# Key pages past the projection: products written to PSUM, pages released by VectorE alone

## The chip, the cores and the metric

One core of a Trainium2 chip runs the whole program; nothing is shared with other cores. The metric is the device time of one execution in microseconds. The kernel before takes 2161.31 us (median of 3 runs, 2160.24 to 2163.03). In the text TensorE is PE in the profile's rows, VectorE is DVE, ScalarE is ACT, GpSimd is POOL and SyncE is SP.

## The reference, cut to what matters

The reference runs one step of a 4-layer decoder trunk for a prompt of 256 tokens and 8 sample sequences that share all weights. Only the attention layer (layer 1) is touched, and of it only the sample side. Each of the 8 samples has one new query of 8 heads x 128 values and 8 past pages of keys (128 positions x 8 heads x 128). What the stretch around the change computes is

```
for n in 8 samples, j in 8 pages, h in 8 heads:
    score[n, j, position, h] = sum over d of key[page_table[n, j], position, h, d] * q[n, h, d]
```

Behind it the page scores are summed by blocks of 256 keys, the three best blocks are kept, a softmax is taken, and the value pages are weighted by it.

## The kernel before, in words

All engines run hand-written queues, tied by semaphores that only count up. The layer projects the input to q, k and v in 12 steps (stage qkv, TensorE). The 64 key pages (t = 8n + j) are loaded one by one by DMAs that GpSimd issues (lines 1323 to 1363): it waits for a free buffer, reads the page's number from the table into a register, and starts a transfer of 512 KB into one of 8 SBUF buffers, pg0 to pg7. A page's 128 positions lie on the 128 partitions, its 8 x 128 values along the free dimension. TensorE spreads the query of sample n over all partitions of two PSUM banks, A[n % 2].

`key_scores(t)` on VectorE (line 1762 on) waits for the page (`s_pg[j]`), multiplies heads 0 to 3 by the query in one instruction (line 1768, counted in `s_km`), and does heads 4 to 7 with one multiply-and-sum each (line 1770, the last counted in `s_kd`). `key_sums(t)` on ScalarE (line 1056 on) waits for `s_km` and sums the products of heads 0 to 3 with four copies that also accumulate (line 1060, the last counted in `s_ka`). Products, and the by-products of the multiply-and-sum, are written over the page itself. After every eighth page VectorE drains, waits until ScalarE has summed this last page, and copies the 64 sums away (line 1776).

A page's buffer is loaded again once both `s_kd` and `s_ka` have counted it (lines 1333 and 1334), so page t follows page t - 8. The eighth sample's key pages (56 to 63) are loaded behind four value pages that go to buffers of their own (pgx). Value pages then reuse the ring.

Pages 0 to 10 are scored between the steps of the projection (`keys_after`, line 346); pages 11 to 63 follow when it is over, one after the other. Two PSUM tensors of two banks each, G[0] and G[1], hold the projection's results, then the rows of k and v of the samples, which ScalarE copies out (`s_row` reaches 3), and lie unused until the scores are complete (`s_kall`, line 1788). TensorE then transposes the scores, and everything else in the layer follows from that.

Of the kernel before, what the change touches and what calls it, by code (L numbers as in the profile page):

```python
# [21 lines left out]
ALU = mybir.AluOpType  # L22
ACT = mybir.ActivationFunctionType
# [3 lines left out]
P = 128  # L27
# [3 lines left out]
NB = 8  # L31
# [13 lines left out]
PAGES = 8  # L45
PGX = 4
# [27 lines left out]
def build_trunk(nc, t_in, t_out):  # L74
# [3 lines left out]
    with ctx:  # L78
# [3 lines left out]
        def sem(name):  # L82
            return ctx.enter_context(nc.semaphore(name))
# [5 lines left out]
        h = sb("h", [P, KT, T])  # L89
# [40 lines left out]
        def row(off, items):  # L130

            got = {}
            for name, shape, *dt in items:
# [4 lines left out]
                if off < x1 and off + n > x0:  # L138
# [46 lines left out]
        pg, m2 = row(m1, [(f"pg{j}", [P, MH, P]) for j in range(PAGES)])  # L185
# [3 lines left out]
        ms, m4 = row(x1, [("sR", [64, 1056]),  # L189
                          ("qk", [P, NB, MH]), ("gsum", [64, BLOCKS]), ("geq", [64, BLOCKS]),  # L190
                          ("gsc", [64, 8]), ("bco", [P, 64]),
                          ("sq0", [P, PAGES, MH]), ("sq1", [P, PAGES, MH])])
# [32 lines left out]
        G = [ctx.enter_context(nc.psum_tensor(f"G{p}", [P, 2, 512], F32)) for p in range(2)]  # L225
# [51 lines left out]
        s_rowT, s_row, s_qbc = sem("s_rowT"), sem("s_row"), sem("s_qbc")  # L277
        s_km, s_ka, s_kd = sem("s_km"), sem("s_ka"), sem("s_kd")
# [67 lines left out]
        def keys_after(r):  # L346

            return range(max(0, 2 * r - 13), 2 * r - 11) if r >= 6 else range(0)

        def mix_count(i):  # L350

# [511 lines left out]
        def _(act):  # L863
            fn = nc.scalar.activation
# [186 lines left out]
            def moba():  # L1051
                def query_rows(j, src):
                    act.wait_ge(s_rowT, j + 1)
                    fn(M["rowS"][:, j, :], src[0:NB].rearrange("b a n -> b (a n)"), ACT.Copy).then_inc(s_row, 1)

                def key_sums(t):
                    n, j = t // PAGES, t % PAGES
                    act.wait_ge(s_km, t + 1)
                    for hh in range(4):
                        f = fn(pg[f"pg{j}"][:, hh, :], pg[f"pg{j}"][:, hh, :], ACT.Copy, accum_out=ms[f"sq{n % 2}"][:, j, hh:hh + 1])  # L1060
                    f.then_inc(s_ka, 1)

                def beside_qkv(r, u):
                    if r == 4:
                        query_rows(0, A[0])
                    for t in keys_after(r):
                        key_sums(t)
                splits(stage[1, "qkv"], beside_qkv, norm=3)
                query_rows(1, G[0])
                query_rows(2, G[1])  # L1070
                for t in range(keys_after(11)[-1] + 1, NB * PAGES):
                    key_sums(t)
                act.wait_ge(s_sR, 1)
                fn(ms["sR"][:, 0:1025], ms["sR"][:, 0:1025], ACT.Exp, scale=SCALE, bias=ms["gsc"][:, 2:3],
                   accum_out=ms["gsc"][:, 3:4]).then_inc(s_sE, 1)

                def weigh(hh):
                    act.wait_ge(s_msc, hh + 1)
                    b = hh % 2
                    sc, nm, rs = mh[f"sc{b}"], mh[f"nm{b}"], mh[f"rs{b}"]  # L1080
                    fn(sc[:, 0:P], sc[:, 0:P], ACT.Exp, scale=SCALE, bias=nm[:, 0:1], accum_out=rs[:, 0:1])
                    fn(sc[:, P:3 * P], sc[:, P:3 * P], ACT.Exp, scale=SCALE, bias=nm[:, 1:2], accum_out=rs[:, 1:2]).then_inc(s_mex, 1)

                def turned(hh):
                    act.wait_ge(s_mpT, hh + 1)
                    if hh >= 2:
                        act.wait_ge(s_mo, hh - 1)
                    fn(mh[f"pt{hh % 2}"][:], pt_bank[:, 0:3 * P], ACT.Copy).then_inc(s_mpt, 1)

                def summed(n):  # L1090
                    act.wait_ge(s_vd, 4 * PAGES * (n + 1))
                    fn(vO[n][:].rearrange("p h d -> p (h d)"), A[n][:].rearrange("p a n -> p (a n)"), ACT.Copy).then_inc(s_vo, 1)
                weigh(0)
                for hh in range(MH):
                    if hh == 4:
                        summed(0)
                    turned(hh)
                    if hh + 1 < MH:
                        weigh(hh + 1)
                act.wait_ge(s_att, 1)  # L1100
                fn(ao["oH"][:, :, 0:SEQ], M["att"][:, :, 0:SEQ], ACT.Copy).then_inc(s_mixh, 1)
                summed(1)
                act.wait_ge(s_att, 2)
                fn(ao["oH"][:, :, SEQ:T], M["att"][:, :, SEQ:T], ACT.Copy).then_inc(s_mixh, 1)
                splits_out(stage[1, "wo"], 4)
# [110 lines left out]
        def _(pool):  # L1216
            gp = nc.gpsimd
# [104 lines left out]
            def moba():  # L1322
                pool.wait_ge(s_ev, stage[1, "qkv"]["c0"])
                pool.dma_start(ptab[:], t_in["page_table"].rearrange("b j -> (b j)").unsqueeze(0)).then_inc(s_tab, 16)
                pool.wait_ge(s_tab, 16)

                def page(pool_dram, t, buf, landed):
                    pid = pool.value_load(ptab[0:1, ds(t, 1)], min_val=0, max_val=pool_dram.shape[1] - 1)
                    pool.dma_start(buf[:], pool_dram[0][ds(pid, 1)].rearrange("o t h d -> t (o h) d")).then_inc(landed, 16)

                def key_page(n, j):
                    if not (isinstance(n, int) and n == 0):
                        pool.wait_ge(s_kd, n * PAGES + (j - 7))
                        pool.wait_ge(s_ka, n * PAGES + (j - 7))
                    page(t_in["cache_k"], n * PAGES + j, pg[f"pg{j}"], s_pg[j])

                def value_page(turn, s):

                    if isinstance(turn, int) and turn == 0:
                        if s >= PGX:  # L1340
                            pool.wait_ge(s_kd, PAGES * (NB - 1) + s - PGX + 1)
                            pool.wait_ge(s_ka, PAGES * (NB - 1) + s - PGX + 1)
                    else:
                        pool.wait_ge(s_vd, turn * RING + (s - RING + 1))
                    page(t_in["cache_v"], turn * RING + s, ring[s], s_px[s] if s < PGX else s_pg[s - PGX])
                for j in range(PAGES):
                    key_page(0, j)
                with gp.Fori(1, NB - 1) as it:
                    for j in range(PAGES):
                        key_page(it, j)  # L1350
                pool.wait_ge(s_mm, stage[1, "qkv"]["g0"] + 12)
                for s in range(PGX):
                    value_page(0, s)
                for j in range(PAGES):
                    key_page(NB - 1, j)
                for s in range(PGX, RING):
                    value_page(0, s)
                turns = NB * PAGES // RING
                with gp.Fori(1, turns) as it:
                    for s in range(RING):  # L1360
                        value_page(it, s)
                for s in range(NB * PAGES - turns * RING):
                    value_page(turns, s)
# [42 lines left out]
        def _(dve):  # L1406
            V = nc.vector
# [348 lines left out]
            def moba():  # L1756
# [5 lines left out]
                def key_scores(t):  # L1762
                    n, j = t // PAGES, t % PAGES
                    page, q, sq = pg[f"pg{j}"], A[n % 2], ms[f"sq{n % 2}"]
                    if j == 0:
                        dve.wait_ge(s_qbc, n + 1)
                    dve.wait_ge(s_pg[j], n * 16 + 16)
                    V.tensor_tensor(page[:, 0:4, :], page[:, 0:4, :], q[:, 0, :].rearrange("p (h d) -> p h d", h=4), ALU.mult).then_inc(s_km, 1)  # L1768
                    for hh in range(4, MH):
                        f = V.tensor_tensor_reduce(page[:, hh, :], page[:, hh, :], q[:, hh // 4, (hh % 4) * P:(hh % 4 + 1) * P],  # L1770
                                                   1.0, 0.0, ALU.mult, ALU.add, sq[:, j, hh:hh + 1])
                    f.then_inc(s_kd, 1)
                    if j == PAGES - 1:
                        dve.drain()
                        dve.wait_ge(s_ka, t + 1)
                        V.tensor_copy(ms["sS"][:, :, n * 8:n * 8 + 8], sq[:])
# [6 lines left out]
                V.tensor_reduce(ms["headsel"][:].rearrange("p m h -> p (m h)"), ident[:].rearrange("p (c r) -> p r c", c=4), AX, ALU.add)  # L1783
                V.memset(pm[:], 0.0)
                V.tensor_tensor(ms["qk"][:], qkv[:, 0:8, S_].rearrange("p h b -> p b h"), qkv[:, 8:16, S_].rearrange("p h b -> p b h"), ALU.mult)
                for t in range(keys_after(11)[-1] + 1, NB * PAGES):
                    key_scores(t)
                dve.drain().then_inc(s_kall, 1)
                sR, gs, geq, gsc = ms["sR"], ms["gsum"], ms["geq"], ms["gsc"]
# [282 lines left out]
```

## Time and profile before

| what | value |
|---|---|
| median of 3 runs | 2161.31 us (2160.24 to 2163.03) |
| the profiled execution, its own time | 2164.97 us |
| its span, first to last instruction | 2163.4 us |
| busy share of the span: PE, DVE, ACT, POOL | 85%, 65%, 43%, 27% |
| key pages past the projection | 737.4 to about 820 us |

The profile is of one execution. An engine's busy share is an average over very different stages; what matters here is the stretch from 737 to 820 us, about 4% of the span. In rows of the timeline the columns are start, length, engine, line, operation, output<-inputs with shapes and count, and, in brackets, how long the engine was idle before and what released it. An instruction's row can overlap the next one's on the same engine, so the pace of an engine is read from start to start.

### The profile page before, as it was taken

The numbers are of one execution on the slowest core, as the hardware profiler recorded it, in microseconds if no ns is written. First come the engines' busy times: TensorE is split into PE (matmuls) and PEld (weight loads), VectorE is DVE, ScalarE is ACT, GpSimd is POOL, SyncE is SP. The second block draws the span as 40 slices with busy tenths as digits, with TensorE's granted clock in tenths as the row PEclk, the third lists the DMA queues.
The fourth block names the chain that finished last, engine by engine and source line by source line (L and its number), as shares of the span: only waits on it lengthen the run. The fifth ranks groups of instructions, "written<-read, shape, count | busy, mean of one in ns | idle before, by whom it ended". The sixth has DMA issues, their size and how long they took to land.

```text
span 2163.4 us, 36660 instructions
## 1 busy us (share of the span) xinstructions
PE 1836.6 (85%) x13205; PEld 1666.5 (77%) x13205; DVE 1416.5 (65%) x2603; ACT 937.8 (43%) x1575; POOL 590.0 (27%) x450
## 2 busy tenths in 40 slices
PE   5998756999989526989998959999899875799997
PEld 4897535999989403389998859999889753699996
DVE  5997977555565895255556775555798778665554
ACT  2455272454333682135434444533445427345432
POOL 2401352243130232334212004411240136134212
PEclk9998856999999757999999979999999875799998
DMA  5454063555547797955554407555355306365550
GB/s 171 137 175 160 17 197 115 185 175 175 175 137 246 239 363 278 374 161 175 175 175 137 159 20 234 182 167 177 114 156 175 126 16 219 114 200 175 177 173 21
DMA packets 317958, 364.87 MB, mean 169 GB/s; under 512 B 7802, under 2 KB 290978, under 8 KB 317750
## 3 DMA queue, kind: packets, MB, share of 16 engines
q1 hardware_dynamic: 296068, 287.41, 42.0%
q0 software_dynamic: 20560, 74.62, 9.5%
q8 instruction: 68, 1.11, 0.2%
q10 hardware_dynamic: 1216, 1.35, 0.2%
q14 instruction: 46, 0.38, 0.1%
HBM read 340.79 MB, written 23.15 MB: 168 GB/s over the span
## 4 chain that ended last, share of the span: by engine, by line
PE 54%; DVE 25%; issue 7%; ACT 5%; DVEq 5%; DMA 2%; POOLq 1%; POOL 1%; ACTq 0%; SPq 0%
PE G L506 16%; PE G L507 15%; PE G L508 15%; DVE wlo L1415 6%; ACT whi L875 2%; DVE out L1719 2%; DVEq L1587 2%; DVE pg L1770 2%; DVE xbc L1585 2%; DVE pg L1768 1%; PE A L735 1%; PE A L472 1%; DVE xL L1476 1%; DVE seg L1673 1%; PE G L593 1%
## 5 line engine op out<-in xcount | busy, mean ns | idle before, releaser
L1415 DVE TENSOR_TENSOR wlo<-raw,whi 128x2048 fp32r<-128x2048 f32 x234 | 545.0, 2329 | 359.4 <-ACT whi L875 359.4
L875 ACT ACTIVATE whi<-raw 128x2048 fp32r<-128x2048 f32 x234 | 447.7, 1913 | 575.0 <-PE G L508 570.5
L506 PE MATMUL G<-xH,whi 128*128 128x264 f32 x2112 | 610.5, 289 | 46.5 <-DVE xL L1476 29.0
L507 PE MATMUL G<-xH,wlo 128*128 128x264 f32 x2112 | 603.4, 286 | 0.0
L508 PE MATMUL G<-xL,whi 128*128 128x264 f32 x2112 | 603.4, 286 | 0.0
L506 PEld LDWEIGHTS G<-xH,whi 128*128 128x128 f32 x2112 | 403.1, 191 | 55.6 <-issue 26.7
L507 PEld LDWEIGHTS G<-xH,wlo 128*128 128x128 f32 x2112 | 403.5, 191 | 0.3
L508 PEld LDWEIGHTS G<-xL,whi 128*128 128x128 f32 x2112 | 401.4, 190 | 0.0
L506 PE MATMUL G<-aH,whi 128*128 128x264 f32 x1024 | 292.2, 285 | 7.9 <-DVE wlo L1415 7.9
L507 PE MATMUL G<-aH,wlo 128*128 128x264 f32 x1024 | 290.8, 284 | 0.0
L508 PE MATMUL G<-aL,whi 128*128 128x264 f32 x1024 | 290.7, 284 | 0.0
L1384 POOL TENSOR_TENSOR ac<-rl 128x528 f32<-128x528 f32 x64 | 167.3, 2614 | 209.7 <-ACT rl L1171 209.7
L506 PEld LDWEIGHTS G<-aH,whi 128*128 128x128 f32 x1024 | 193.5, 189 | 9.0 <-DVE wlo L1415 9.0
L507 PEld LDWEIGHTS G<-aH,wlo 128*128 128x128 f32 x1024 | 193.7, 189 | 0.0
L508 PEld LDWEIGHTS G<-aL,whi 128*128 128x128 f32 x1024 | 192.7, 188 | 0.0
L1249 POOL TENSOR_TENSOR sums<-h 128x528 f32<-128x528 f32 x39 | 61.8, 1585 | 363.3 <-DVE xg L1466 353.4
L1247 POOL TENSOR_TENSOR sums<-h 128x528 f32<-128x528 f32 x13 | 21.8, 1675 | 350.6 <-DVE xg L1466 338.6
L1585 DVE SCALAR_TENSOR_TENSOR xbc<-T,colC,xbc 128x256 f32 (+1 forms) x192 | 94.1, 531 | 11.8 <-issue 8.3
L1060 ACT ACTIVATE pg<-pg 128x128 f32<-128x128 f32 x256 | 75.9, 297 | 33.7 <-DVE pg L1768 31.6
L1312 POOL TENSOR_TENSOR stt<-stt,out 128x2048 f32 (+1 forms) x16 | 72.4, 4526 | 62.8 <-DVE out L1707 60.5
L1993 DVE TENSOR_TENSOR aL<-ac,aH 128x528 f32 (+1 forms) x64 | 45.4, 709 | 65.7 <-POOL ac L1384 65.0
L1289 POOL TENSOR_TENSOR xde<-xd,tm 128x256 f32<-128x256 f32 x32 | 18.9, 611 | 239.1 <-DVE cbm L1662 239.1
(377 smaller groups left out, 3272.2 us busy)
## 6 DMA issues: line engine op xcount, KB each, us to landing
raw<-in_mlp_w_up SPq DMA_DIRECT2D x64, 1024.0 KB, 5.6
raw<-in_mlp_w_down SPq DMA_DIRECT2D x64, 1024.0 KB, 5.2
raw<-in_ssd_w_in SPq DMA_DIRECT2D x48, 1024.0 KB, 5.4
pg<-in_cache_k POOLq DMA_DIRECT2D x64, 512.0 KB, 5.5
pg<-in_cache_v POOLq DMA_DIRECT2D x40, 512.0 KB, 6.4
raw<-in_ssd_w_out SPq DMA_DIRECT2D x16, 1024.0 KB, 5.2
out_ssd_state_s<-stt SPq DMA_DIRECT2D x16, 1024.0 KB, 4.7
raw<-in_ple_w_gate SPq DMA_DIRECT2D x16, 1024.0 KB, 5.2
```

The costliest lines, as they stand in the source:

```text
L506: mm(o, whi[u % 2][:, k, w], act_h[:, x, :], start=first, stop=False)
L507: mm(o, wlo[u % 2][:, k, w], act_h[:, x, :], start=False, stop=False)
L508: done = mm(o, whi[u % 2][:, k, w], act_l[:, x, :], start=False, stop=last)
L875: fn(whi[u % 2][:], raw[(u + 2) % 4][:], ACT.Copy).then_inc(s_hi, 1)
L1060: f = fn(pg[f"pg{j}"][:, hh, :], pg[f"pg{j}"][:, hh, :], ACT.Copy, accum_out=ms[f"sq{n % 2}"][:, j, hh:hh + 1])
L1249: gp.tensor_tensor(hh2, hr, hr, ALU.mult)
L1312: gp.tensor_tensor(st_, st_, otm[f"out{b}"][:].rearrange("p t n -> p (t n)"), ALU.add).then_inc(s_hn, 1)
L1384: gp.tensor_tensor(ml[f"ac{b}"][:], ml[f"rl{b}"][:], ml[f"rl{b}"][:], ALU.mult).then_inc(s_ac, 1)
L1415: V.tensor_tensor(wlo[u % 2][:], raw[(u + 2) % 4][:], whi[u % 2][:].bitcast(F32), ALU.subtract).then_inc(s_lo, 1)
L1585: f = V.scalar_tensor_tensor(o, T_[:, t, k:k + SEQ], colC[:, q, ds(tile + k * CT, 1)], o, ALU.mult, ALU.add)
L1587: dve.drain()
L1993: V.tensor_tensor(aL[:, ds(r * 2, 2), :], ml[f"ac{b}"][:], aH[:, ds(r * 2, 2), :].bitcast(F32), ALU.subtract).then_inc(s_aL, 1)
```

## The change

`beside` is the first page scored past the projection, 11. For pages below it nothing changes but where GpSimd's loop begins. For pages 11 to 63:

- VectorE's products go to G[0][:, t % 2, :] and the by-products of line 1770 to G[1][:, t % 2, :], one PSUM bank each, in turn for even and odd pages. The page is only read.
- Ahead of each page VectorE also waits until `s_ka` and `s_kd` have counted page t - 2, whose bank it writes again. Before the first of them it waits for `s_row` 3.
- ScalarE reads the products from the PSUM bank and writes its copies back there.
- GpSimd loads a page's buffer again when `s_kd` alone has counted it. The loads of samples 1 and 2 are written out in full, and the loop begins at sample 3.

```
+        beside = keys_after(11)[-1] + 1
...
                     act.wait_ge(s_km, t + 1)
+                    w = pg[f"pg{j}"][:, 0:4, :] if t < beside else G[0][:, t % 2, :].rearrange("p (h d) -> p h d", h=4)
                     for hh in range(4):
-                        f = fn(pg[f"pg{j}"][:, hh, :], pg[f"pg{j}"][:, hh, :], ACT.Copy, accum_out=ms[f"sq{n % 2}"][:, j, hh:hh + 1])
+                        f = fn(w[:, hh, :], w[:, hh, :], ACT.Copy, accum_out=ms[f"sq{n % 2}"][:, j, hh:hh + 1])
...
                         pool.wait_ge(s_kd, n * PAGES + (j - 7))
-                        pool.wait_ge(s_ka, n * PAGES + (j - 7))
+                        if isinstance(n, int) and (n - 1) * PAGES + j < beside:
+                            pool.wait_ge(s_ka, n * PAGES + (j - 7))
...
                             pool.wait_ge(s_kd, PAGES * (NB - 1) + s - PGX + 1)
-                            pool.wait_ge(s_ka, PAGES * (NB - 1) + s - PGX + 1)
...
-                with gp.Fori(1, NB - 1) as it:
+                for n in (1, 2):
+                    for j in range(PAGES):
+                        key_page(n, j)
+                with gp.Fori(3, NB - 1) as it:
...
-                    V.tensor_tensor(page[:, 0:4, :], page[:, 0:4, :], q[:, 0, :].rearrange("p (h d) -> p h d", h=4), ALU.mult).then_inc(s_km, 1)
+                    if t < beside:
+                        w, spare = page[:, 0:4, :], page[:, 4:8, :]
+                    else:
+
+                        dve.wait_ge(s_ka, t - 1)
+                        dve.wait_ge(s_kd, t - 1)
+                        w, spare = (G[a][:, t % 2, :].rearrange("p (h d) -> p h d", h=4) for a in range(2))
+                    V.tensor_tensor(w, page[:, 0:4, :], q[:, 0, :].rearrange("p (h d) -> p h d", h=4), ALU.mult).then_inc(s_km, 1)
                     for hh in range(4, MH):
-                        f = V.tensor_tensor_reduce(page[:, hh, :], page[:, hh, :], q[:, hh // 4, (hh % 4) * P:(hh % 4 + 1) * P],
+                        f = V.tensor_tensor_reduce(spare[:, hh - 4, :], page[:, hh, :], q[:, hh // 4, (hh % 4) * P:(hh % 4 + 1) * P],
...
-                for t in range(keys_after(11)[-1] + 1, NB * PAGES):
+                dve.wait_ge(s_row, 3)
+                for t in range(beside, NB * PAGES):
                     key_scores(t)
```

## Rows read from the trace of the kernel before

**Rows 1.** Busy time by stage: stretch, length, busy (x instructions), TensorE clock, DMA share, GB/s

```profile
core 0: us, PE busy (x) PEld busy (x) DVE busy (x) ACT busy (x) POOL busy (x), PEclk, DMA share, GB/s
745.28:806.03 60.75, 18.32 (x20) 5.31 (x18) 58.20 (x366) 51.13 (x320) 21.94 (x42) 0.50 0.97 349
```

**Rows 2.** The chain that ended last, 736 to 760 us, by line

```profile
by line: DVE pg L1770 42.4%; DVE pg L1768 38.2%; ACT pg L1060 10.7%; DVE pm L1784 7.4%; DVE sq L1770 1.7%; issue 1.0%; DVE qk L1785 0.3%; DVE sS L1776 0.3%; DVEq L1774 0.1%
```

**Rows 3.** Timeline of VectorE: page 23, the eighth of its sample, and page 24

```profile
755.29 0.68 DVE L1768 TENSOR_TENSOR pg<-pg,A 128x512 f32<-128x512 f32 x1
...
755.89 0.28 DVE L1770 CUSTOM_DVE_ANT_0 pg<-pg,A 128x128 f32<-128x128 f32 x1
...
756.10 0.28 DVE L1770 CUSTOM_DVE_ANT_0 pg<-pg,A 128x128 f32<-128x128 f32 x1
...
756.73 0.08 DVE L1770 DVE_READ_ACCUMULATOR2_ANT sq<- 128x1 f32 x1
...
757.32 0.20 DVE L1776 COPY sS<-sq 128x64 f32<-128x64 f32 x1 [0.51 <-ACT pg L1060]
757.43 0.68 DVE L1768 TENSOR_TENSOR pg<-pg,A 128x512 f32<-128x512 f32 x1
```

**Rows 4.** Timeline of ScalarE for the same page 23

```profile
756.01 0.31 ACT L1060 ACTIVATE pg<-pg 128x128 f32<-128x128 f32 x1
...
756.32 0.29 ACT L1060 ACTIVATE pg<-pg 128x128 f32<-128x128 f32 x1
...
757.10 0.19 ACT L1060 ACTIVATION_READ_ACCUMULATOR pg<-pg 128x1 f32 x1
```

**Rows 5.** Waits, 737 to 820 us: who for whom, total us, times, longest

```profile
DVE sS L1776 <- ACT pg L1060: 3.6, 7, 0.5
...
DVE pg L1768 <- DMA pg<-in_cache_k: 1.5, 1, 1.5
```

**Rows 6.** Timeline of GpSimd: issues of page 55, four value pages, pages 56, 57

```profile
795.08 0.53 POOL L1329 DMA_DIRECT2D pg<-in_cache_k  x1 [0.91 <-issue]
...
798.99 0.53 POOL L1329 DMA_DIRECT2D pgx<-in_cache_v  x1 [0.92 <-issue]
800.13 0.53 POOL L1329 DMA_DIRECT2D pgx<-in_cache_v  x1 [0.61 <-issue]
801.35 0.53 POOL L1329 DMA_DIRECT2D pg<-in_cache_k  x1 [0.70 <-DVE sq L1770]
802.57 0.53 POOL L1329 DMA_DIRECT2D pg<-in_cache_k  x1 [0.69 <-DVE sq L1770]
```

**Rows 7.** Timeline: VectorE's and ScalarE's last rows on page 47

```profile
793.17 0.08 DVE L1770 DVE_READ_ACCUMULATOR2_ANT sq<- 128x1 f32 x1
...
793.55 0.18 ACT L1060 ACTIVATION_READ_ACCUMULATOR pg<-pg 128x1 f32 x1
```

**Rows 8.** The chain, 790 to 810 us, in order: start, us, what

```profile
793.05 0.20 DVE pg L1770
793.27 0.38 issue
793.65 0.14 POOL pg L1329
...
801.35 6.13 DMA pg<-in_cache_k
```

**Rows 9.** Groups of VectorE by shape: count, busy us, mean ns

```profile
L1743 DVE TENSOR_TENSOR yL<-zs,yH 128x528 fp32r<-128x528 f32 x16 | 11.2, 703 | 0.4 <-ACT yH L1041 0.4
L1627 DVE TENSOR_TENSOR zs<-G,rstd 128x528 f32<-128x528 f32 x16 | 11.2, 700 | 1.4 <-PE G L508 1.4
```

**Rows 10.** Groups of ScalarE by shape: count, busy us, mean ns

```profile
L1171 ACT ACTIVATE rl<-G 128x528 f32<-128x528 f32 x64 | 37.9, 592 | 0.0
L899 ACT ACTIVATE xH<-xg 128x528 fp32r<-128x528 f32 x32 | 20.4, 638 | 58.1 <-DVE xg L1466 58.1
```

**Rows 11.** Timeline where the projection ends and page 11 begins

```profile
735.39 1.90 ACT L1054 ACTIVATE rowS<-G 8x1024 f32<-8x1024 f32 x2
...
737.43 0.67 DVE L1768 TENSOR_TENSOR pg<-pg,A 128x512 f32<-128x512 f32 x1
```

## The prediction, as put on record

> **What bounds the kernel now.** I first read the profile by stage. While the key pages are scored past the projection, VectorE is busy 58.20 of 60.75 us, ScalarE 51.13, and TensorE only 18.32, at half clock, for the queries that it spreads [rows 1]. The DMAs move 349 GB/s there. Then the chain that ended last: from 736 to 760 us the two lines of VectorE on the pages hold 42.4% and 38.2% of it, ScalarE's sums 10.7% [rows 2]. So the change lies on the path that sets the end, and what it saves or costs in this stretch moves all that follows, since TensorE begins the next step only when the last page is scored.
>
> Next the timeline of one page. Counting from start to start, VectorE spends 755.29 to 755.89, so 0.60 us, on the product of four heads, and 0.21 us (755.89 to 756.10) on each of the four multiply-and-sums: 0.60 + 4 x 0.21 = 1.43 us [rows 3]. Nothing waits between them. ScalarE begins at 756.01 and ends at 757.10 + 0.19 = 757.29, so 1.28 us per page: it fits under VectorE's 1.43 [rows 4]. Only at each eighth page does it show: VectorE's last row ends at 756.81 (756.73 + 0.08), the copy of the sums starts at 757.32, right behind ScalarE's end, and 0.51 us were idle [rows 3, 4]. There are 7 such waits past the projection, 3.6 us in all, and one wait for a load, 1.5 us [rows 5].
>
> That one load is on the chain. VectorE ends page 47 at 793.17 + 0.08 = 793.25, ScalarE at 793.55 + 0.18 = 793.73 [rows 7]. That frees the buffer for page 55, issued at 795.08, 1.35 us behind ScalarE. Four value pages follow in the queue, then page 56 at 801.35 [rows 6]. It takes 6.13 us to land [rows 8], and VectorE stands 1.5 us for it. The chain goes from VectorE's page 47 through GpSimd's queue to that load [rows 8]. So pages 48 to 55 have a cover of 1.5 us, and what VectorE gains or loses in them does not count until that is used up. Exposed are 53 - 8 = 45 pages.
>
> **VectorE's own instructions.** Per page 5 of them change their output from SBUF to PSUM; their count and inputs stay. No VectorE row of this trace has a PSUM output. The nearest rows are those that differ in an input alone: 128x528 elements take 703 ns from SBUF and 700 ns with an input in PSUM [rows 9]. From these I take 0 for the output too. The outer bound is the only place where the memory changes a duration: ScalarE takes 592 ns with its input in PSUM and 638 ns with it in SBUF, 46 ns apart [rows 10]. That bounds each instruction at +-46 ns, so +-0.23 us per page.
>
> The Trainium skill speaks against this change twice. Its page "VectorE: DVE Perf Modes" (section "The TRN2 errata") gives a VectorE instruction 58 fixed cycles from SBUF to SBUF but 120 from PSUM to SBUF, and "Advanced Engine Details and Errata" (section "The Read-Write Bubble") says that VectorE is closer to SBUF and ScalarE to PSUM. For VectorE's inputs the trace does not agree (700 against 703 ns); for its outputs no run here shows it. If the 62 cycles held for an output, an estimate by that page would be 65 ns per instruction and some 0.3 us per page.
>
> **The two added waits per page.** They stand in front of the product, behind them in VectorE's queue the rest of the page, and for that ScalarE and GpSimd wait. Both events are long past: VectorE's page t - 2 ended 1.43 us before, and ScalarE's page ends 757.29 - 755.29 = 2.00 us after its product began, 0.86 us short of two pages (2 x 1.43). The sequencer's own time for a wait is not shown apart, but between the copy at 757.32 and the product at 757.43 two waits are passed in 0.11 us [rows 3]. Today's one wait per page costs nothing: the product follows the last multiply-and-sum at its usual 0.21 us. I take 0, as three waits at 0.055 us fit into that 0.21. The upper bound is 0.11 us per page; a wait can't give time back. Exposed on 45 pages it is 5.0 us, as 8 x 0.11 = 0.9 on pages 48 to 55 stays under the cover.
>
> The wait for the copied rows of k and v ahead of page 11: ScalarE's two copies end at 735.39 + 1.90 = 737.29, and VectorE starts page 11 at 737.43 anyway [rows 11]. I take 0, with at most 0.1.
>
> **ScalarE.** Its input moves to PSUM: 4 x 46 ns = 0.18 us less per page [rows 10]. That is hidden under VectorE but for the eighth pages. What the output in PSUM does is not shown; bounds of -46 and +46 ns per instruction make the 0.18 either 0.36 or 0. Waits at pages 15, 23, 31 and 39 lie ahead of page 47, those of pages 47 and 55 under the load's cover, and that of page 63 counts again: 5 x 0.18 = 0.9 us. What is late next there is still ScalarE, with 0.51 - 0.18 = 0.33 us left.
>
> **GpSimd.** Without ScalarE's release page 55 is issued as much earlier as VectorE ends page 47 before ScalarE does: 793.73 - 793.25 = 0.48 us [rows 7], at least 0 if the queue itself was late. One wait less ahead of page 56: with two waits the issues are 1.22 us apart, without 1.14 [rows 6], so 0.04. All other loads are freed earlier as well, but are not waited for. The load of page 56 then lands 4 x 0.18 + 0.52 = 1.2 us earlier, and VectorE arrives 6 x 0.18 = 1.1 earlier, so it still stands there for about 1.3 us. The loops written out at samples 1 and 2 change no order; 0. The value pages for the ring come earlier too, and are used only behind the softmax: 0.
>
> **The sum.** 0.9 + 0.48 + 0.04 = 1.4 us saved. Against the profiled execution's own time, 2164.97 us (span 2163.4 and 1.6 around it), that is 2163.6. That execution is 3.7 us above the median; carried over to the median, 2161.31 - 1.4 = 2159.9 us. The forecast's own range: nothing saved at all gives 2161.3; all of five waits gone (5 x 0.51 = 2.6) and 0.5 from the load gives 2158.2.
>
> **The rivals.**
>
> Slower: a PSUM output costs VectorE time on every instruction. It is then no longer ScalarE's place or the release that matters, but 5 instructions x 45 pages on the chain. At the bound of 46 ns that is 0.23 x 45 = 10.4 us, and pages 48 to 55 add 8 x 0.23 - 1.3 = 0.5: 2159.9 + 10.9 = 2170.8 us. It eats up the saving from 1.4 / 225 = 6 ns per instruction, and makes the kernel slower by over 0.2% (4.3 us, about what a measurement of this kernel can tell from no change) from (1.4 + 4.3) / 225 = 25 ns. For it: no row shows such an output, the banks it writes lie beside those that it reads the query from, and every multiply-and-sum would alternate between an output in PSUM and its sum in SBUF. Against it: inputs show no such difference. The skill's fixed cycles, above, are this rival at a higher price; an estimate by that page is 17 us for 265 instructions. Chance 0.21, spread between 2165 and 2177.
>
> Waits exposed: the sequencer can't pass three waits in the time of one multiply-and-sum. 5.0 us: 2164.9, still within 0.2%. Against it speaks the 0.11 us for two. Chance 0.08.
>
> Faster: a PSUM output frees VectorE's next instruction sooner. At 20 ns it is 0.1 x 45 = 4.5 us: 2155.4. It can't go far: the loads already run at 349 GB/s [rows 1], and four value pages and page 56 were issued 1.14 to 1.45 us apart and still took 6.13 us to land, so VectorE would soon wait for pages. Chance 0.12.
>
> The release doesn't do what it says: page 55 is issued no earlier, because GpSimd's queue was the late one (the chain has it busy with the issue before, at 793.65, when page 47 ends). Then 0.9 us remain, 2160.4; that lies in the forecast's range and is counted there. Together with the forecast: chance 0.59.
>
> **How the numbers follow.** Likeliest, 2159.9. The range has to reach to the rivals until 2 in 10 are left out: below to 2156 (half of the faster case), above to 2170 (of the slower case about 0.11 lies beyond). Faster by over 0.2% (below 2157.0): the faster case, 0.12. Slower by over 0.2% (above 2165.6): 0.21. Within: 0.59 + 0.08 = 0.67.
>
> **What would show it.** In the profile after: the product still 0.60 us from start to start and each multiply-and-sum 0.21 (else the PSUM output has a price, read there directly); no idle time ahead of the product except at page 56 (else the waits); ScalarE's rows about 250 ns where they are 290 now, and the copy of the sums 0.33 us behind VectorE in place of 0.51; page 56's load still waited for, some 1.3 us. The prediction is wrong if the start-to-start time of a page is not 1.43 us, since 10 ns on it are already 0.5 us.

## The result, and the profile after

The changed kernel took 2168.3 us (median of 12 runs, 2163.77 to 2169.42), the kernel before 2162.86 us beside it (12 runs, 2160.24 to 2166.68). The ratio is 1.0021, with a 95% interval of 1.0012 to 1.0030: some 4.5 us slower, between 2.6 and 6.5. (The ratio goes by all runs; the two medians alone lie 5.4 us apart.) The forecast was 1.4 us faster. The time lies inside the stated range, but on the side that was given 0.21.

The stage that answers to [rows 1], from the profile of the changed kernel (columns as there), and the chain from 736 to 760 us that answers to [rows 2]:

```profile
745.28:806.03 60.75, 18.89 (x20) 5.80 (x20) 59.34 (x334) 44.25 (x292) 20.23 (x39) 0.50 0.91 318
```

```profile
by line: DVE G L1783 39.9%; DVE G L1781 23.6%; DVE sq L1783 10.3%; ACT G L1063 10.2%; issue 9.3%; DVE pm L1797 7.2%; DVEq L1787 0.5%; DVEq L1779 0.4%; DVE sS L1789 0.3%
```

VectorE is busier (59.34 us for 58.20) with fewer instructions (334 for 366), and the DMAs moved 318 GB/s for 349: it gets through fewer pages in the same 60.75 us. The sum reads alone (`sq L1783`) now hold 10.3% of the chain, for 1.7% before, and "issue", time for which the profile shows no wait, 9.3% for 1.0%. What these shares mean the timeline has to say. The groups of the stretch 737 to 826 us by shape (count, busy us, mean ns, idle before):

```profile
L1783 DVE CUSTOM_DVE_ANT_0 G<-pg,A 128x128 f32<-128x128 f32 x212 | 54.6, 320 | 0.0
L1781 DVE TENSOR_TENSOR G<-pg,A 128x512 f32<-128x512 f32 x53 | 38.5, 727 | 0.0
L1783 DVE DVE_READ_ACCUMULATOR2_ANT sq<- 128x1 f32 x212 | 30.1, 142 | 0.0
L1789 DVE COPY sS<-sq 128x64 f32<-128x64 f32 x7 | 1.4, 205 | 2.0 <-ACT G L1063 2.0
```

Each of these rows lasts longer than the step to the next row, so the durations overlap and don't add up. The starts in the timeline do. VectorE in the changed kernel, page 23 and the start of page 24, the same two as in [rows 3] (start us, duration us; a multiply-and-sum is two rows, the CUSTOM one and the read of its sum):

```profile
757.13 0.73 DVE L1781 TENSOR_TENSOR G<-pg,A 128x512 f32<-128x512 f32 x1
757.77 0.28 DVE L1783 CUSTOM_DVE_ANT_0 G<-pg,A 128x128 f32<-128x128 f32 x1
757.97 0.14 DVE L1783 DVE_READ_ACCUMULATOR2_ANT sq<- 128x1 f32 x1
757.97 0.33 DVE L1783 CUSTOM_DVE_ANT_0 G<-pg,A 128x128 f32<-128x128 f32 x1
758.22 0.14 DVE L1783 DVE_READ_ACCUMULATOR2_ANT sq<- 128x1 f32 x1
758.22 0.33 DVE L1783 CUSTOM_DVE_ANT_0 G<-pg,A 128x128 f32<-128x128 f32 x1
...
758.72 0.14 DVE L1783 DVE_READ_ACCUMULATOR2_ANT sq<- 128x1 f32 x1
759.14 0.20 DVE L1789 COPY sS<-sq 128x64 f32<-128x64 f32 x1 [0.28 <-ACT G L1063]
759.32 0.69 DVE L1781 TENSOR_TENSOR G<-pg,A 128x512 f32<-128x512 f32 x1
759.92 0.29 DVE L1783 CUSTOM_DVE_ANT_0 G<-pg,A 128x128 f32<-128x128 f32 x1
```

The first multiply-and-sum still takes 0.20 us from start to start (757.77 to 757.97). The second takes 0.25 (757.97 to 758.22), and so do the third and the fourth. The product takes 0.64 (757.13 to 757.77), but 0.60 where the copy stands ahead of it (759.32 to 759.92). A page is 0.64 + 0.20 + 3 x 0.25 = 1.59 us for 1.43, the first of a sample 1.55. A sum read lasts 0.14 us for 0.08. No row inside the page shows idle time ahead of it.

From the start of page 11 to the copy behind page 63 it took 82.20 us before (737.43 to 819.63) and takes 87.91 now (737.56 to 825.47), 5.71 more. The steps account for it: of 46 steps from page to page inside a sample, 39 are longer by 0.16 and 7 by 0.12, so 7.1 us. Five steps over a sample's end are 2.19 us for 2.14 (757.13 to 759.32), 0.25 in all. And the step into page 56 is 2.18 us for 3.69, so 1.5 less, because its load has landed by now. 7.1 + 0.25 - 1.5 = 5.8, the 5.71 but for rounding.

ScalarE on page 23, as in [rows 4]:

```profile
757.90 0.26 ACT L1063 ACTIVATE G<-G 128x128 f32<-128x128 f32 x1 [0.37 <-DVE G L1781]
...
758.16 0.27 ACT L1063 ACTIVATE G<-G 128x128 f32<-128x128 f32 x1
...
758.92 0.18 ACT L1063 ACTIVATION_READ_ACCUMULATOR G<-G 128x1 f32 x1
```

It takes 757.90 to 759.10, so 1.20 us for 1.28. GpSimd's issues of page 55, the third value page and page 56, and VectorE's last row on page 47, answering to [rows 6] and [rows 7]:

```profile
798.51 0.15 DVE L1783 DVE_READ_ACCUMULATOR2_ANT sq<- 128x1 f32 x1
...
799.94 0.53 POOL L1332 DMA_DIRECT2D pg<-in_cache_k  x1 [1.06 <-issue]
...
803.56 0.53 POOL L1332 DMA_DIRECT2D pgx<-in_cache_v  x1 [0.62 <-issue]
...
805.86 0.53 POOL L1332 DMA_DIRECT2D pg<-in_cache_k  x1 [0.63 <-DVE sq L1783]
```

Page 55 is issued 799.94 - 798.66 = 1.28 us behind VectorE, for 1.83 before (795.08 - 793.25). The release did move. Page 56 also follows page 55 sooner: 5.92 us (799.94 to 805.86) for 6.27 (795.08 to 801.35). The 0.92 us of idle time ahead of the third value page in [rows 6] is 0.62 here.

### The profile page after: what moved, and what is told of

It is laid out like the page before. It is cut to its first block, busy times and chain, and to the rows that moved or that the text cites. A ratio compares the mean times of both kernels' runs of the same rounds, so it can differ in the third digit from the quotient of the medians.

```text
span 2167.0 us, 36627 instructions
## 1 busy us (share of the span) xinstructions
PE 1833.8 (85%) x13205; PEld 1667.7 (77%) x13205; DVE 1424.1 (66%) x2603; ACT 934.7 (43%) x1575; POOL 591.0 (27%) x450
## 4 chain that ended last, share of the span: by engine, by line
PE 53%; DVE 25%; issue 7%; ACT 5%; DVEq 5%; POOLq 1%; DMA 1%; POOL 1%; ACTq 0%; SPq 0%
PE G L508 16%; PE G L509 15%; PE G L510 15%; DVE wlo L1421 6%; ACT whi L877 2%; DVE out L1725 2%; DVEq L1593 2%; DVE G L1783 2%; DVE xbc L1591 2%; PE A L474 1%; DVE xL L1482 1%; DVE G L1781 1%; DVE seg L1679 1%; PE A L737 1%; DVE xg L1472 1%
## 5 line engine op out<-in xcount | busy, mean ns | idle before, releaser
L1027 ACT ACTIVATE stt<-stt,hv x256 | 75.2, 385 | 7.2 <-DMA stt<-in_state_ssd 7.2
```

The costliest lines, as they stand in the source:

```text
L1027: f = fn(blk, blk, ACT.Copy, scale=hv2["hv"][:, t, ds(n + 8, 1)])
```

## The experiments

Four theories stood at the start; the expectations give letters to three. A: an instruction with its output in PSUM pays when it stands right behind one with its output in SBUF, as behind each sum read. B: a short instruction with its output in PSUM pays behind another short one, whatever the memory of the sums. C: the added waits cost the time. The fourth, without a letter: the release by VectorE alone costs or gives something. Each run below is set against runs of the kernel before on the same chip. "Page" is a page inside a sample from start to start, "stretch" runs from the start of page 11 to the copy behind page 63 (the first of three copies in the kernel with three sums in PSUM). Pages and stretches come from one profiled execution of each kernel, times and ratios from 10 to 12 runs.

A stretch of one execution is good to about half a microsecond only, because the load of page 56 doesn't always take as long. From its issue to the start of page 56 it took 6.23 us in the profile of before, 5.52 with the waits alone and 5.81 in the run with a delay below, which has the code of before in the whole stretch. That stretch is 81.79 us (736.17 to 817.96), for 82.20.

| kernel | page, us | stretch, us | us, before beside it | ratio (95%) |
|---|---|---|---|---|
| before | 1.43 | 82.20 | | |
| the change | 1.59 | 87.91 | 2168.3, 2162.86 | 1.0021 (1.0012 to 1.0030) |
| waits alone | 1.43 | 81.83 | 2164.34, 2164.3 | 1.0000 (0.9991 to 1.0009) |
| three sums in PSUM | 1.43 | 82.10 | 2163.51, 2164.3 | 0.9991 (0.9981 to 1.0000) |
| products alone in PSUM | 1.43 | 81.35 | 2161.61, 2164.3 | 0.9986 (0.9977 to 0.9995) |
| by-products alone in PSUM | 1.55 | 86.70 | 2168.57, 2164.3 | 1.0021 (1.0011 to 1.0030) |
| side buffers in SBUF | 1.43 | 81.52 | 2161.55, 2162.88 | 0.9992 (0.9983 to 1.0001) |
| release by both | 1.59 | 88.20 | 2168.93, 2162.88 | 1.0026 (1.0017 to 1.0035) |

**The waits alone.** The kernel before with the added waits:

```diff
+                    if t >= keys_after(11)[-1] + 1:
+                        dve.wait_ge(s_ka, t - 1)
+                        dve.wait_ge(s_kd, t - 1)
                     V.tensor_tensor(page[:, 0:4, :], page[:, 0:4, :], ...
...
+                dve.wait_ge(s_row, 3)
                 for t in range(keys_after(11)[-1] + 1, NB * PAGES):
```

> The kernel before, with only the added waits of the change: ahead of each page from 11 on VectorE waits for s_ka and s_kd to have counted page t - 2, and for s_row 3 ahead of page 11. All outputs stay in SBUF and both releases stay. Theory A (an instruction with its output in PSUM loses 0.04 us when it stands right behind one with its output in SBUF): a page stays at 1.43 us from start to start, time within 2 us of before. Theory C (the waits make the 0.16 us per page): 1.59 us per page, 6 us slower.

The page stayed at 1.43 us and the ratio is 1.0000. The stretch is even 0.37 us shorter, since the load was waited for by 0.7 us here and not by 1.5. Only behind the copy do the waits show. VectorE on a sample's last page and the next:

```profile
754.51 0.68 DVE L1771 TENSOR_TENSOR pg<-pg,A 128x512 f32<-128x512 f32 x1
...
756.54 0.20 DVE L1779 COPY sS<-sq 128x64 f32<-128x64 f32 x1 [0.52 <-ACT pg L1060]
756.72 0.69 DVE L1771 TENSOR_TENSOR pg<-pg,A 128x512 f32<-128x512 f32 x1
```

The product starts 0.18 us behind the copy's start (756.54 to 756.72), for 0.11 in [rows 3]: 0.07 for two waits, once in eight pages. The same 0.18 stands in the changed kernel. The waits (C) fall as the cause.

**Three sums in PSUM too.** The changed kernel, but from sample 2 on the sums of heads 4 to 6 go to spare columns of a PSUM bank, and head 7 has by-product and sum in SBUF:

```diff
+                        total_ = sq[:, j, hh:hh + 1]
+                        by = spare[:, hh - 4, :]
+                        if n >= 2:
+                            c = 3 * P + 12 * (n % 2) + 3 * (j // 2) + hh - 4
+                            if hh < 7:
+                                total_ = G[1][:, j % 2, c:c + 1]
+                            else:
+                                by = page[:, hh, :]
```

> The changed kernel, but from sample 2 on the sums of heads 4 to 6 go to PSUM as well, next to their by-products; head 7 keeps by-product and sum in SBUF. Theory A (change of output memory): only the product, behind head 7's sum in SBUF, is late; 0.64 for it, 0.21 for each multiply-and-sum, 1.47 us per page. Theory B (each short instruction with its output in PSUM costs 0.04 us more behind another short one): heads 5 and 6 still take 0.25, 1.55 us per page or more. By A it is 4 to 5 us faster than the changed kernel and level with before.

VectorE in it:

```profile
754.48 0.69 DVE L1781 TENSOR_TENSOR G<-pg,A 128x512 f32<-128x512 f32 x1
755.08 0.29 DVE L1791 CUSTOM_DVE_ANT_0 G<-pg,A 128x128 f32<-128x128 f32 x1
755.28 0.10 DVE L1791 DVE_READ_ACCUMULATOR2_ANT G<- 128x1 f32 x1
755.28 0.30 DVE L1791 CUSTOM_DVE_ANT_0 G<-pg,A 128x128 f32<-128x128 f32 x1
...
755.49 0.30 DVE L1791 CUSTOM_DVE_ANT_0 G<-pg,A 128x128 f32<-128x128 f32 x1
...
755.70 0.29 DVE L1791 CUSTOM_DVE_ANT_0 pg<-pg,A 128x128 f32<-128x128 f32 x1
755.90 0.09 DVE L1791 DVE_READ_ACCUMULATOR2_ANT sq<- 128x1 f32 x1
755.90 0.70 DVE L1781 TENSOR_TENSOR G<-pg,A 128x512 f32<-128x512 f32 x1
```

With four large outputs of five in PSUM the page is back at 1.42 us (754.48 to 755.90), 1.43 over the stretch. Pages 11 to 15 of the same trace still have their sums in SBUF, and take 1.58. So B falls: a PSUM output has no price of its own here. It is the alternation that costs, though not in the form of A: the product at 755.90 stands right behind a sum read into SBUF, was expected to pay for that (1.47 us a page), and does not. The by-products and sums of these rows share one PSUM bank, and nothing is late; the late product of the change goes to another bank than the by-product ahead of it. So writing the same bank twice in a row isn't the cause either.

**Only the products in PSUM.** The changed kernel with its by-products written over the page, as before:

```diff
-                        w, spare = (G[a][:, t % 2, :].rearrange("p (h d) -> p h d", h=4) for a in range(2))
+                        w, spare = G[0][:, t % 2, :].rearrange("p (h d) -> p h d", h=4), page[:, 4:8, :]
```

> The changed kernel with the by-products of heads 4 to 7 written over the page again, in SBUF; the products stay in PSUM, the release by s_kd alone stays. Theory A: one change from SBUF to PSUM per page, 1.47 us per page, 1.8 us lost on 45 pages against 1.4 us saved: within 2 us of before. Theory B: the product alone is long, so 0.60 + 4 x 0.21 = 1.43 us, and 1.4 us faster than before. ScalarE's page is shorter (about 1.20 us against 1.28) by both.

VectorE, a sample's last page and the next:

```profile
757.62 0.69 DVE L1781 TENSOR_TENSOR G<-pg,A 128x512 f32<-128x512 f32 x1
758.22 0.28 DVE L1783 CUSTOM_DVE_ANT_0 pg<-pg,A 128x128 f32<-128x128 f32 x1
...
758.43 0.28 DVE L1783 CUSTOM_DVE_ANT_0 pg<-pg,A 128x128 f32<-128x128 f32 x1
...
759.05 0.09 DVE L1783 DVE_READ_ACCUMULATOR2_ANT sq<- 128x1 f32 x1
759.59 0.20 DVE L1789 COPY sS<-sq 128x64 f32<-128x64 f32 x1 [0.45 <-ACT G L1063]
759.77 0.69 DVE L1781 TENSOR_TENSOR G<-pg,A 128x512 f32<-128x512 f32 x1
```

The page is 1.43 us, 0.60 and 0.21 as in [rows 3]; A had it at 1.47. This kernel shows what the rest of the change is worth once VectorE's price is gone: the stretch is 0.85 us shorter, where I had forecast 1.4 for it. The step into page 56 is 2.79 us for an eighth page's 2.15, so its load is still waited for by 0.64 us. Before, that step was 3.69 us: the whole gain of the stretch is this load.

**Only the by-products in PSUM.** The kernel before with one wait and the by-products moved:

```diff
-                        f = V.tensor_tensor_reduce(page[:, hh, :], page[:, hh, :], ...
+                        by = page[:, hh, :] if t < 11 else G[1][:, t % 2, (hh - 4) * P:(hh - 3) * P]
+                        f = V.tensor_tensor_reduce(by, page[:, hh, :], ...
```

> The kernel before with only the by-products of heads 4 to 7 in PSUM from page 11 on (with a wait for VectorE's own page t - 2 and for s_row 3); products and ScalarE stay in SBUF, both releases stay. Theory A: all four multiply-and-sums stand behind an SBUF output (the product, then three sums): 0.60 + 4 x 0.25 = 1.59 us per page, 5 us slower than before. Theory B: the first follows a long instruction and stays 0.21, so 1.55.

```profile
752.74 0.68 DVE L1770 TENSOR_TENSOR pg<-pg,A 128x512 f32<-128x512 f32 x1
753.34 0.29 DVE L1773 CUSTOM_DVE_ANT_0 G<-pg,A 128x128 f32<-128x128 f32 x1
...
753.55 0.33 DVE L1773 CUSTOM_DVE_ANT_0 G<-pg,A 128x128 f32<-128x128 f32 x1
...
753.79 0.33 DVE L1773 CUSTOM_DVE_ANT_0 G<-pg,A 128x128 f32<-128x128 f32 x1
...
754.04 0.33 DVE L1773 CUSTOM_DVE_ANT_0 G<-pg,A 128x128 f32<-128x128 f32 x1
754.29 0.14 DVE L1773 DVE_READ_ACCUMULATOR2_ANT sq<- 128x1 f32 x1
754.29 0.69 DVE L1770 TENSOR_TENSOR pg<-pg,A 128x512 f32<-128x512 f32 x1
```

These rows of VectorE give 0.60 + 0.21 + 3 x 0.25 = 1.55 us within rounding (752.74 to 753.34, 753.55, 753.79, 754.04, 754.29), where A had 1.59, and the kernel is as slow as the whole change, within the intervals. The product at 754.29 writes to SBUF beside a long sum read (0.14 us) and lasts its usual 0.69: in this kernel the late ones are heads 5 to 7, three a page, and in the whole change the product is the fourth.

**Which neighbour it takes.** The kernel before with by-products in PSUM for heads 4 and 5 on even pages, 5 and 7 on odd ones (one execution, 2164.35 us):

```diff
+                        by = page[:, hh, :] if t < 11 or hh not in ((4, 5), (5, 7))[t % 2] else G[1][:, t % 2, (hh - 4) * P:(hh - 3) * P]
```

> The kernel with only by-products in PSUM, thinned out: on even pages those of heads 4 and 5, on odd pages those of heads 5 and 7; the others, all products and all sums go to SBUF. If an output in PSUM is late only where the instruction before its predecessor's sum wrote PSUM too (PSUM, sum in SBUF, PSUM), even pages take 0.04 us more (head 5), 1.47 us, and odd pages 1.43. If the step from an SBUF by-product were enough, both would take more.

An even page, then an odd one, on VectorE:

```profile
757.22 0.69 DVE L1770 TENSOR_TENSOR pg<-pg,A 128x512 f32<-128x512 f32 x1
757.82 0.29 DVE L1773 CUSTOM_DVE_ANT_0 G<-pg,A 128x128 f32<-128x128 f32 x1
...
758.03 0.33 DVE L1773 CUSTOM_DVE_ANT_0 G<-pg,A 128x128 f32<-128x128 f32 x1
...
758.28 0.28 DVE L1773 CUSTOM_DVE_ANT_0 pg<-pg,A 128x128 f32<-128x128 f32 x1
...
758.70 0.68 DVE L1770 TENSOR_TENSOR pg<-pg,A 128x512 f32<-128x512 f32 x1
...
759.50 0.29 DVE L1773 CUSTOM_DVE_ANT_0 G<-pg,A 128x128 f32<-128x128 f32 x1
...
759.92 0.29 DVE L1773 CUSTOM_DVE_ANT_0 G<-pg,A 128x128 f32<-128x128 f32 x1
...
760.13 0.68 DVE L1770 TENSOR_TENSOR pg<-pg,A 128x512 f32<-128x512 f32 x1
```

The even page takes 1.48 us (757.22 to 758.70), and the odd one 1.43 (758.70 to 760.13) with as many PSUM outputs; over the stretch they are 1.47 and 1.43. Only head 5 of the even page is long (0.33 for 0.28 or 0.29). So the rule, as far as these runs go: an instruction with its output in PSUM costs 0.04 us more when it stands right behind a sum read into SBUF whose own multiply-and-sum wrote its by-product to PSUM. PSUM, SBUF, PSUM costs; one change of memory does not. The last part of the rule was told apart by this one execution, on 26 pages of each kind. The change has 4 such places per page, by-products alone 3, this kernel 1 on every other page, and products alone or three sums in PSUM none: 1.59, 1.55, 1.47 and 1.43 us.

**Side buffers without PSUM.** The changed kernel with its products in two idle SBUF buffers and its by-products over the page. It separates the second buffer and the earlier release from PSUM:

```diff
-                        w, spare = (G[a][:, t % 2, :].rearrange("p (h d) -> p h d", h=4) for a in range(2))
+                        w, spare = mh[f"kvt{t % 2}"][:], page[:, 4:8, :]
```

> The changed kernel with its products in two spare SBUF buffers (in turn for even and odd pages) and its by-products over the page, so the release by VectorE alone and the added waits stay, and no output is in PSUM. What is left of the theories: only a PSUM output behind a sum whose own by-product went to PSUM is late. So 1.43 us per page. ScalarE's page is back at 1.28 us, the copy of the sums 0.51 us behind VectorE; the load of page 56 comes up to 0.5 us earlier, the added waits cost 0.06 us at each eighth page. In sum the last page is scored 0.1 to 0.5 us earlier than before, time within 2 us of before. If it is 3 us faster as the kernel with only the products in PSUM was, the release alone is what gains.

1.43 us a page, a stretch of 81.52, and a ratio whose interval touches 1. Without any output in PSUM, page 56 is issued 7.19 us behind VectorE's page 47, for 8.10 before, and the added waits behind the copies take 0.35 us of that back. So the release, with the loops written out, gives some 0.7 us of the stretch at most, and costs nothing.

**The release by both.** The changed kernel, with GpSimd waiting for ScalarE's page as before:

```diff
-                        if isinstance(n, int) and (n - 1) * PAGES + j < beside:
-                            pool.wait_ge(s_ka, n * PAGES + (j - 7))
+                        pool.wait_ge(s_ka, n * PAGES + (j - 7))
```

> The changed kernel with one part undone: GpSimd again waits for ScalarE too before it loads a page. Pages at 1.59 us. If the release by VectorE alone gains nothing here: the last page as late as in the changed kernel (5.8 us later than before) and the same time, 4 to 5 us above before. If it gains 1 to 2 us further on, as the medians so far hint, this is 1 to 2 us slower than the changed kernel, ratio to before 1.0026 to 1.003.

The page is 1.59 us again, and the stretch 0.29 longer than with the change, 88.20 for 87.91. The intervals around 1.0026 and 1.0021 overlap: the release doesn't make the 4.5 us. The issues show what it does. Page 55 is issued 1.59 us behind VectorE's page 47, for 1.28 in the change, and page 56 follows 5.98 us later (801.76 to 807.74), for 5.92. So of the 0.35 us by which that gap shrank in the change the wait makes 0.06. The gap is 5.90 to 5.98 us in each kernel that has the first loops written out and the value pages where they were, and 6.26 to 6.30 in each that has the loop of before; why, no run shows.

**Does a delay here reach the end?** The kernel before with three drains and memsets of `pm` behind the last page:

```diff
+                for _ in range(3):
+                    dve.drain()
+                    V.memset(pm[:], 0.0)
                 dve.drain().then_inc(s_kall, 1)
```

> The kernel before with a delay: three more fills of pm on VectorE, each behind a drain, between the last page and the event that TensorE waits for (1.8 us each, 5.3 us together; nothing else changes). If a delay of the scores moves all that follows one for one: 5.3 us slower, ratio 1.0025. If the value stage gives some of it back because its first loads have landed: about 2 us slower.

```profile
818.68 1.76 DVE L1790 MEMSET pm<- 128x2048 f32 x1 [0.53 <-issue]
820.98 1.76 DVE L1790 MEMSET pm<- 128x2048 f32 x1 [0.53 <-issue]
823.27 1.76 DVE L1790 MEMSET pm<- 128x2048 f32 x1 [0.53 <-issue]
```

In the trace each took 1.76 + 0.53 = 2.29 us, so I had put in 6.9 us, not the 5.3 expected. The kernel took 1.0041 of the time (1.0026 to 1.0056; 4 runs), 5.6 to 12.1 us more. So at least 5.6 of the 6.9 us arrive, and the case of only 2 us is out. In the two profiles of before and after, the first row of the value stage is 5.85 us later (835.14 to 840.99) and the end only 3.6. The length from there to the first row of the next residual differs from execution to execution: 103.0 us in the profile of before, 100.3 in that of the change. In the five executions that score late, with a value stage at 838.8 us or later, it is 98.8 to 100.9; in the nine others 99.8 to 103.6, 1.4 us more in the mean. So some microsecond may be given back there, but single executions that scatter by 4 us don't show it. 5.7 us at the end of the stretch, passed on whole or nearly, fit the 2.6 to 6.5 that were measured.

**A version that is faster?** Only the products in PSUM; of the added waits only the one that they need, and not at a sample's first page; and the four value pages, which stood ahead of page 56, issued one by one among the key pages of samples 3 to 6. GpSimd's wait for the end of the projection now stands ahead of sample 3:

```diff
-                with gp.Fori(3, NB - 1) as it:
-                    for j in range(PAGES):
-                        key_page(it, j)
                 pool.wait_ge(s_mm, stage[1, "qkv"]["g0"] + 12)
-                for s in range(PGX):
-                    value_page(0, s)
+                for n in range(3, NB - 1):
+                    for j in range(PAGES):
+                        key_page(n, j)
+                        if j == 3:
+                            value_page(0, n - 3)
...
-                        dve.wait_ge(s_ka, t - 1)
-                        dve.wait_ge(s_kd, t - 1)
+                        if j:
+                            dve.wait_ge(s_ka, t - 1)
```

> The kernel with only the products in PSUM, with two more edits: of the added waits only the one for ScalarE is kept, and not at a sample's first page; and the four value pages that stood between the loads of pages 55 and 56 go one by one between the key pages of samples 3 to 6. Page 56 is then not waited for (0.6 us of idle time gone against that kernel), and 0.06 us less at each of 7 eighth pages: last page 1 us earlier than there, 2 us earlier than before. Time 1 to 4 us below before. If the loads moved in delay key pages, VectorE shows waits for DMA in samples 3 to 6.

The load of page 56 is no longer waited for (step into it 2.09 us, for 3.69), an eighth page takes 2.08 for 2.14, and the stretch is 80.25 us, 1.95 shorter. The kernel took 2161.9 us for 2162.88, a ratio of 0.9993 (0.9984 to 1.0002). As so little is hard to tell from none, three kernels ran once more.

> The changed kernel again, unaltered, on the chip of the two below. 1.59 us per page, 4 to 6 us above before.

> The kernel with only the products in PSUM again. The trace puts its last page 1 us ahead of before and 6.5 us ahead of the change, so by the stretch alone 1 us below before; its first comparison gave 3 us. If that was luck: 0.9991 to 1.0 now.

> The kernel with only the products in PSUM and the four value pages' loads moved, again. The trace puts its last page 1 us ahead of the one above, so 2 us below before: 0.9988 to 0.9995.

The change: 2168.12 us for 2163.62, 1.0023 (1.0014 to 1.0032), with a stretch of 87.92 us. Products alone: 2162.01 us for 2163.62, 0.9991 (0.9982 to 1.0000). With the loads moved: 2161.75 for 2163.62, 0.9984 (0.9975 to 0.9993). The stretch with the loads moved is 80.25 us again. So the change is slower again, and both versions lie at or just under the kernel before, by 0.7 to 1.6 parts in a thousand with the loads moved. Which of the two is better the intervals do not say.

## Why the prediction was wrong

**What bounds it: right.** Page times in this stretch do set the end. 5.7 us there came out as about 4.5, and of a delay of 6.9 us at least 5.6 arrived.

**VectorE's outputs: the step that failed.** I gave 0 for an output in PSUM, by the nearest rows, 703 and 700 ns [rows 9]. These rows differ in an input and have no second output. For a lone large output that 0 was even right: the product in PSUM takes 0.60 us. But a multiply-and-sum has two outputs, and the pair was split between two memories. I had written that very thing down as an argument for the slower rival, and then priced all five instructions alike and weighed the rival by the inputs. It was the term that a row of an input can't bound. Measured it is 0.16 us a page, 32 ns for each of the five instructions, against the outer bound of 46 and the 25 from which the rival said slower. The prediction's own sign, a page that isn't 1.43 us, came true with 1.59. The rival's sum was 10.4 + 0.5 us; with 0.16 for 0.23 it would have been 7.2 for the 45 exposed pages, less the 1.4 saved 5.8, and the stretch grew by 5.7. That this agrees so well is in part luck: of the 1.4 nothing came from ScalarE, a page at a sample's end lost 0.05 and not 0.16, and the 1.5 us of waiting for page 56 went, as the cover said.

In the Trainium skill's page "VectorE: DVE Perf Modes" (section "The TRN2 errata") a PSUM source has 62 fixed cycles more than an SBUF source, an estimate of 65 ns by that page; had it held for the output, a product in PSUM would take longer, and it takes 0.60 us in either memory. The sign that the Trainium skill gives in "Advanced Engine Details and Errata" (section "The Read-Write Bubble": VectorE closer to SBUF) came true for the whole kernel, but at 0.04 us where the outputs alternate and at nothing where they do not. The Trainium skill also says in "VectorE: DVE Perf Modes" (section "Two Vector instructions with no wait between them") when an instruction is held until all earlier ones are done: when its first input from a memory, or its output, starts in another group of 32 partitions than the last instruction's on that memory. All rows here cover 128 partitions, so by that rule nothing is held, and indeed each late instruction starts before the one ahead has ended (758.22 against 757.97 + 0.33 = 758.30). So the 0.04 us are no hold of that kind.

**The added waits: right but for the eighth pages.** 0 inside a page (ratio 1.0000). Behind the short copy they cost 0.07 us at each of the six copies that a product follows, five of them exposed: 0.35 us, for which I had 0. The product starts 0.21 us behind the last multiply-and-sum, and 0.11 behind the copy, so it seems that the step from the instruction ahead covers the waits; no run tests that apart.

**ScalarE: mechanism right, size off.** With the data in PSUM its rows fell from 297 to 265 ns in the mean, where I had 46 ns each and so 0.18 us a page. But its page went from 1.28 to 1.20 us only: from start to start the first ACTIVATE of a page fell from 0.31 to 0.26 or 0.27 us, the others only from 0.29 to 0.28 or 0.29, as a sum read stands between them and the durations overlap. 5 x 0.08 = 0.4 us, not 0.9, and the 0.07 behind the copy took nearly all of that: an eighth page costs 2.15 us with the products alone in PSUM, for 2.14.

**GpSimd: one term near, one missed.** Page 55 was issued 0.55 us nearer to VectorE's page 47 (1.28 for 1.83 us), forecast 0.48. But page 56 followed it 0.35 us sooner (5.92 for 6.27), where I had 0.04 for the wait and 0 for the loops written out; the wait makes 0.06. The load of page 56 would still have been waited for, forecast 1.3 us: 0.64 with the products alone, and 0.16 when that kernel ran again (a step of 2.31; the page behind it was late by another 0.3), so this wait varies by some half a microsecond for one and the same kernel. In the change itself it vanished, because VectorE came later.

**The sum.** 1.4 us were to be saved. The products alone, which are the change without the term that failed, saved 0.85 us of the stretch, and 1.0 when run again (81.18). That is near the 1.4, but by other terms: about 0 for ScalarE's 0.9, and 0.55 + 0.35 = 0.90 for the 0.52 of the load. By the times these kernels were 3.0 and 1.9 us faster (1.1 to 5.0, 0 to 3.9). The sign was lost by one term of 7.1 us.

## What to carry to other kernels

Before an output is moved to PSUM, look whether the instruction has a second one, a sum or an accumulator, and keep both in one memory where several such instructions stand in a row; a product without a sum could go either way here. Where no row shows an output, a row of an input says nothing of it, and the term needs a chance of its own, by how often it comes on the chain: at the change's 265 instructions, 0.03 us each outweigh all else that this change did. Read the cost of an instruction from start to start, not from its duration, on ScalarE as on VectorE.

## What the runs showed of the hardware

A multiply-and-sum on 128x128 elements takes 0.21 us on VectorE with both outputs in SBUF, both in PSUM, or mixed with SBUF outputs around it, and 0.25 us between by-products in PSUM when the sums go to SBUF. A sum read behind a by-product in PSUM lasts 0.14 us into SBUF, 0.09 or 0.10 into PSUM, and 0.08 to 0.09 behind a by-product in SBUF. Whether a write still under way to PSUM holds up the sum read, and the sum read then holds up the next write to PSUM, would fit all of it; but this is not shown, and no run tells it from another cause inside the engine.

Two waits cost VectorE nothing behind an instruction of 0.21 us and 0.07 us behind a copy that starts 0.11 us ahead. ScalarE's ACTIVATE with its sum gets 32 ns shorter as a row with its data in PSUM, but at most 10 ns from start to start, except for the first of a page (0.26 or 0.27 for 0.31). With the same data in side buffers in SBUF both are as before, 0.31 and 0.29.
